# Turning normed rows over six PSUM banks, and the odd low halves of a layer norm on GpSimd

## What is computed

```python
h = rms_norm(h + merged @ w_out, norm_ffn)          # then h @ w_ffn_in: stage "ffn"
h = layer_norm(x, ln_in_g, ln_in_b)
for l in range(2):
    proj = h @ w_in[l]                              # stage "in" of layer l
    ...                                             # attention, mix
    h = layer_norm(ALPHA * h + mix, ln1_g[l], ln1_b[l])
    q = h @ wq[l]                                   # stage "exp" of layer l, then the experts
    ...
    h = layer_norm(ALPHA * h + ffn, ln2_g[l], ln2_b[l])
```

## Time and profile before

| what | value |
|---|---|
| median of 3 runs | 2452.79 us (2447.13 to 2454.69) |
| the profiled execution | 2454.43 us |
| its span, first to last instruction | 2452.6 us |
| mean granted clock of TensorE | 0.988 |
| TensorE busy | 2392.8 us (98%) |
| VectorE busy | 1676.7 us (68%) |
| ScalarE busy | 1264.9 us (52%) |
| GpSimd busy | 541.3 us (22%) |

### The profile page before, as it was taken

One profiled execution on the slowest core, in us unless ns is written; L12 is line 12 of the kernel. 1 busy time (PEld: TensorE's weight loads), 2 busy tenths in 40 slices (PEclk: granted clock), 3 DMA queues, 4 the chain that ended last, 5 costly groups with the idle time before them and its releaser, 6 DMA issues. The chain is left out here.

```text
span 2452.6 us, 42445 instructions
## 1 busy us (share of the span) xinstructions
PE 2392.8 (98%) x16695; PEld 2173.9 (89%) x16695; DVE 1676.7 (68%) x3016; ACT 1264.9 (52%) x2699; POOL 541.3 (22%) x423
## 2 busy tenths in 40 slices
PE   7999999999999999999999999999999999999997
PEld 7888989998889999999888878789999999888886
DVE  4737345446779767887777556769776888777556
ACT  6542335445655545445555555655554455555553
POOL 3640224545278200000000002368400000000000
PEclk9999999999899999999999999999999999999999
DMA  5320145554145566666777664245656666777664
GB/s 181 124 85 17 40 150 172 188 186 139 70 151 180 182 181 192 195 194 199 239 245 224 196 207 152 95 129 165 188 181 190 194 195 194 229 243 236 195 199 144
DMA packets 148068, 420.98 MB, mean 172 GB/s; under 512 B 15904, under 2 KB 49056, under 8 KB 147488
## 3 DMA queue, kind: packets, MB, share of 16 engines
q1 hardware_dynamic: 144080, 405.34, 52.8%
q0 software_dynamic: 2192, 8.99, 1.0%
q10 hardware_dynamic: 1600, 3.96, 0.5%
HBM read 400.40 MB, written 17.83 MB: 171 GB/s over the span
## 5 line engine op out<-in xcount | busy, mean ns | idle before, releaser
L1142 ACT CAST hi<-raw 128x512 fp32r<-128x512 f32 x1402 | 818.6, 620 | 379.9 <-PE pb L439 227.6
L439 PE MATMUL pb<-HTh,hi 128*128 128x256 f32 (+1 forms) x2968 | 857.6, 289 | 2.6 <-POOL lo L2377 1.9
L439 PE MATMUL pb<-HTl,hi 128*128 128x256 f32 (+1 forms) x2968 | 840.8, 283 | 0.0
L439 PE MATMUL pb<-HTh,lo 128*128 128x256 f32 (+1 forms) x2968 | 840.5, 283 | 0.0
L2377 POOL TENSOR_TENSOR lo<-raw,hi 128x512 fp32r<-128x512 f32 x383 | 520.7, 1383 | 542.1 <-ACT hi L1142 541.7
L1660 DVE TENSOR_TENSOR lo<-raw,hi 128x1024 fp32r<-128x1024 f32 x464 | 565.0, 1218 | 85.7 <-ACT hi L1142 85.5
L439 PEld LDWEIGHTS pb<-HTh,hi 128*128 128x128 f32 x2968 | 568.6, 192 | 7.2 <-issue 2.8
L439 PEld LDWEIGHTS pb<-HTl,hi 128*128 128x128 f32 x2968 | 569.1, 192 | 1.0
L439 PEld LDWEIGHTS pb<-HTh,lo 128*128 128x128 f32 x2968 | 568.6, 192 | 0.0
L439 PE MATMUL pb<-hi,WH 128*128 128x512 f32 x1112 | 433.5, 390 | 5.0 <-DVE WL L2341 4.9
L439 PE MATMUL pb<-lo,WH 128*128 128x512 f32 x1112 | 432.9, 389 | 0.0
(11 more groups left out here) (197 smaller groups left out, 2155.2 us busy)
## 6 DMA issues: line engine op xcount, KB each, us to landing
raw<-in_uT SPq DMA_DIRECT2D x256, 512.0 KB, 3.6
raw<-in_vT SPq DMA_DIRECT2D x256, 512.0 KB, 3.7
raw<-in_w_ffn_in SPq DMA_DIRECT2D x44, 512.0 KB, 4.0
raw<-in_wq SPq DMA_DIRECT2D x32, 512.0 KB, 3.5
wk<-kept SPq DMA_DIRECT2D x128, 128.0 KB, 3.8
raw<-in_w_in SPq DMA_DIRECT2D x24, 512.0 KB, 3.7
raw<-in_w_ffn_out SPq DMA_DIRECT2D x22, 512.0 KB, 4.3
raw<-in_w_gate SPq DMA_DIRECT2D x16, 512.0 KB, 3.3
```

The costliest lines, as they stand in the source:

```text
L439: return e.matmul(o, l, r, start=start, stop=stop)
L1142: e.copy(u.hi[k], u.half[k]).then_inc(*s.up("hi", ("hi", g)))
```

## The change

The table `NORMED` gives each kind of stage six banks and one spare bank for filler. On PE a new function `turned_normed` takes the place of `turned` in all five stages: chunks 0 to 5 go to six different banks, so none of them waits for a reader. Then come 8 filler matmuls, chunk 6 (first bank again), 3 filler matmuls, chunk 7 (second bank again) and 3 filler matmuls, and then the product. That is 14 filler matmuls in each stage that were not there.

In `in` and `exp`, POOL gets the low halves of the odd chunks 1, 3, 5, 7 (`turned_low`), ahead of its splits for the stage; DVE keeps those of 0, 2, 4, 6. ACT takes out the odd chunks 1, 3, 5 as before, and chunk 7 goes from ACT to DVE, which takes it out when `turn` of chunk 5 is there and its own low half of chunk 6 is done. Who waited for `turn` of chunk 7 now waits for that of 6 too, as the two are counted on different semaphores.

```diff
+NORMED = {"ffn": ((1, 2, 3, 4, 5, 6), 7), "in": ((0, 1, 2, 3, 6, 7), 5), "exp": ((2, 3, 4, 5, 6, 7), 1)}
...
+    def turned_normed(kind, tag, src, ready, done):
+
+        banks, other = NORMED[kind]
+        for c in range(8):
+            b = banks[c % 6]
+            if c == 6:
+                warm(other, 8)
+            elif c == 7:
+                warm(other, 3)
+            emptied(b)
+            for t in range(2):
+                w.wait_ge(*s.to(*ready(t, c // 4)))
+                x = tp(PB[b][:, t * 128:(t + 1) * 128], src[:, t, c * 128:(c + 1) * 128])
+            x.then_inc(*s.up("turn_ps", ("turn_ps", tag, c)))
+            free[b] = [(step, tag, c) for step in done]
+        warm(other, 3)
...
-    turned("ffn", m.XN, lambda t, k: ("xn1", t, k), range(8), FOUR)
+    turned_normed("ffn", "ffn", m.XN, lambda t, k: ("xn1", t, k), ("turn",))
...
-        turned(("in", l), m.Hv, lambda t, k: ("hn", 2 * l, t, k), range(8), FOUR, low=False)
+        turned_normed("in", ("in", l), m.Hv, lambda t, k: ("hn", 2 * l, t, k), ("biased",))
...
-        turned(("exp", l), m.Hv, lambda t, k: ("hn", 2 * l + 1, t, k), range(8), FOUR, low=False)
+        turned_normed("exp", ("exp", l), m.Hv, lambda t, k: ("hn", 2 * l + 1, t, k), ("biased",))
...
     def turned_biased(tag, gain, bias, prev):
 
+        banks = NORMED[tag[0]][0]
         for c in range(8):
-            p, h, ty = PB[c % 4][:, 0:256], m.HT[0][:, c, :], m.TY[c % 2]
-            if c % 2:
+            p, h, ty = PB[banks[c % 6]][:, 0:256], m.HT[0][:, c, :], m.TY[c % 2]
+            if c in (1, 3, 5):
                 w.wait_ge(*s.to("turn_ps", tag, c))
                 if c > 1:
                     w.wait_ge(*s.to("turn", tag, c - 2))
...
         def low(c):
             w.wait_ge(*s.to("turn_hi", tag, c))
-            x = tt(m.HT[1][:, c, :], m.TY[c % 2], m.HT[0][:, c, :].bitcast(F32), S)
-            x.then_inc(*up("turn", ("turn", tag, c), *(done if c == 7 else ())))
-
-        for c in range(8):
-            if c % 2 == 0:
-                w.wait_ge(*s.to("turn_ps", tag, c))
-                own()
-                ts(m.TY[0], PB[c % 4][:, 0:256], K(gain, c), K(bias, c), M, A).then_inc(*up("biased_dve", ("biased", tag, c)))
-            if c:
-                low(c - 1)
-        low(7)
+            x = tt(m.HT[1][:, c, :], m.TY[0], m.HT[0][:, c, :].bitcast(F32), S)
+            x.then_inc(*up("turn", ("turn", tag, c), *(done if c == 6 else ())))
+
+        banks = NORMED[tag[0]][0]
+        for c in (0, 2, 4, 6, 7):
+            w.wait_ge(*s.to("turn_ps", tag, c))
+            if c == 7:
+                w.wait_ge(*s.to("turn", tag, 5))
+            own()
+            ts(m.TY[c % 2], PB[banks[c % 6]][:, 0:256], K(gain, c), K(bias, c), M, A).then_inc(*up("biased_dve", ("biased", tag, c)))
+            if c < 7:
+                low(c)
...
+    def turned_low(tag):
+
+        for c in (1, 3, 5, 7):
+            w.wait_ge(*s.to("turn_hi", tag, c))
+            tt(m.HT[1][:, c, :], m.TY[1], m.HT[0][:, c, :].bitcast(F32), S).then_inc(*s.up("turn_pool", ("turn", tag, c)))
+
     for l in range(2):
+        turned_low(("in", l))
...
+        turned_low(("exp", l))
         for a in range(16):
             take("wq", l, a)
```

More of the change, by code:

```diff
@@ L1427, in scalar @@
     fn(sm[:, 64:66], sm[:, 62:64], ACT.Sqrt).then_inc(*s.up("roots", ("root1",)))
-    turned("ffn", range(8), FOUR, "norm_ffn")
+    turned("ffn", range(8), NORMED["ffn"][0], "norm_ffn")
     def ffn_in(j):
@@ L1577, in scalar @@
                 w.wait_ge(*s.to("key_ps", l, a - 2))
+            w.wait_ge(*s.to("turn", ("exp", l), 6))
             w.wait_ge(*s.to("turn", ("exp", l), 7))
@@ L1988, in gain_step @@
         w.wait_ge(*s.to("turn_ps", tag, 7))
+        w.wait_ge(*s.to("turn", tag, 6))
         w.wait_ge(*s.to("bc", n))
@@ L2432, in gpsimd @@
                 take("win", l, i, g)
+        w.wait_ge(*s.to("turn", ("in", l), 6))
         w.wait_ge(*s.to("turn", ("in", l), 7))
```

## The result

The change makes the kernel slower. Its median is 2461.34 us (2456.42 to 2463.74, 5 runs) against 2450.32 us of the kernel before, which five runs now have; the ratio is 1.0042, with an interval of [1.0026, 1.0058]. That is 6 to 14 us, where +2.9 us was forecast. In a second timing on another occasion it was 1.0048 [1.0035, 1.0062]. The median also lies 0.34 us over the upper end of the range. The forecast gave 91% to a change within 0.3%, and 1.0042 lies above that. That the median came so near the range is in part luck: the forecast started from a median of 2452.79 us, which five runs put at 2450.32. The two medians differ by 11.0 us, so the change itself was missed by 8.1 us, the time by 5.6 us only. And the two profiled executions differ by just 2.0 us.

The account below looks back on a forecast made before the run. The prediction took TensorE, busy 98% of the span, as the bound. Terms of +0.5 (`ffn`), +4.1 (`exp`) and -1.7 us (`in`) summed to +2.9: 2457.3 profiled, 2455.7 us as median, range 2449 to 2461.

Parts of the forecast that it names:

- The waits: In `exp`, TensorE's first product waits for chunk 3 until +4.65, 5 until +6.5 and 7 until +8.35 us.
- GpSimd's price: A 128x256 low half on POOL in `in` and `exp`: 0.72 us, with 0.45 and 1.26 as the ends.
- the longer chain: In `exp`, a pair of chunks takes 1.88 us instead of 1.55; the first product ends 0.6 us later.
- the half clock of `exp`: In each `exp`, 15 matmuls at 0.214 us instead of 0.12, later than before: 1.4 us.
- Transposes and filler: TensorE's transposes and filler take 3.8 to 4.0 us in each stage; in `ffn` this costs 0.5 us.
- `exp`, the term mis-sized: The two `exp` stages: later product end and half clock cost 2.0 us each, +4.1 us together.
- The rival that the clock holds: In `exp` the clock stays up despite the waits; the time is 2452.8 us; chance 17%.
- Term 3: The two `in` stages: no half clock, a 0.8 us wait for weights; gain 0.84 us each, -1.7 together.
- The base: Whole kernel: the profiled execution took 2454.43 us and the median of the runs lies 1.64 us below it.
- The rival on the slower side: POOL takes 1.26 us a low half in `in` and `exp`: +11.5 us, 2464.3 us; chance 5%.

Follow-up runs that it names:

- r9: The changed kernel with 39 instead of 3 filler matmuls behind chunk 7 in `exp`; 2456.74 us, ratio 1.0033 to the kernel before.
- r3: The changed kernel with four banks and no filler as before, keeping GpSimd's low halves and chunk 7 on VectorE; 2454.29 us, ratio 1.0027.
- r4: The change in the two `in` stages only, `ffn` and `exp` as in the kernel before; 2451.14 us, ratio 1.0017.
- r7: The change in the two `exp` stages only, `ffn` and `in` as in the kernel before; 2459.39 us, ratio 1.0038.
- r2: The changed kernel with six banks and filler, but all low halves on VectorE and chunk 7 on ScalarE as before; 2448.91 us, ratio 0.9991.
- r8: As r2, but `ffn` with four banks as before and 20 filler matmuls behind chunk 7 in `exp`; 2447.76 us, ratio 0.9994.
- r1: The changed kernel once more, without edit; 2458.62 us, ratio 1.0048 to the kernel before.

## Why the forecast was too low

The waits, GpSimd's price, the longer chain and the half clock of `exp` are in the traces where the forecast placed them. The gain in `in` is not there against the usual trace of before, and the sum was too small.

- **GpSimd's price** (0.72 taken, between 0.45 and 1.26): 0.72 to 0.74 measured. Right. That it contends with DVE was said but not priced: DVE's low halves beside it took 0.74 instead of 0.43, which put the last chunk at +8.71 and not at +8.3. The GPSIMD Engine Reference of the Trainium skill (Key points) names just this case, VectorE instructions with two SBUF inputs; the trace agrees with it. Its factor of about two for GpSimd (Engine selection) is 1.7 here, 0.73 against 0.43 us.
- **Transposes and filler.** 3.5 us from the first transpose to the product in `exp` (688.84 to 692.29) where 3.9 was taken; 3.2 in `in`. So `ffn` lost 0.15 us (9.57 against 9.42 to ACT's first step on the product), not 0.5. In `in`, on the other hand, TensorE came to the fifth chunk 0.35 us earlier than forecast and the weights 0.37 us later (+10.00 against +9.63), so it waited 1.57 us, not 0.8.
- **`exp`, the term mis-sized.** +2.0 each was forecast, +3.0 is the mean (15.2 of ten occurrences against 12.2), and +3.3 the usual value. The longer chain costs 1.1 (forecast 0.6). The half clock cost 2.2 (forecast 1.4): I let it last for 3.2 us of full work as in the trace of before, but it began before the last wait, and after that wait it lasted from 698.83 to 703.9, 5.1 us and 24 matmuls, not 15. The rival that the clock holds came true in one `exp` of ten.
- **`in`, the step that failed.** Term 3 was a gain of 0.84 us each, from half clock that the filler would take away. The forecast compared with a stage at half clock, since both `in` of the only trace had it. The other traces show it in one of six. With the clock up before, the stage took 14.4 us, and the change, which waits for weights instead, takes 15.6 to 15.8. Against the mean of the eight (15.0) the term is +0.7 each and not -0.84. I counted it as a gain that filler would bring, while it is mostly there without filler.
- **The base.** I corrected the profiled execution by 1.64 us to the median of three runs. Some 50 further runs of before had medians of 2448.3 to 2449.9, so the profiled execution of 2454.43 lies 4.5 to 6 us over the usual one.

The sum with the measured terms is 0.15 + 2 x 0.7 + 2 x 3.0 = 7.6 us, ratio 1.0031. It lies in the first interval [1.0026, 1.0058], a little under the second [1.0035, 1.0062]. Behind the first ffn transpose the three traces of the change are on the mean 6.0 us longer than the three of before (2078.3 against 2072.3), and 6.5 us longer (1884.5 against 1878.0) if the attention, which scatters with the clock, is taken off. That is near the 7.6, from three traces each.

Some 3 us of the timed difference are not accounted for. In r9 it is alike: 2 x 0.7 + 2 x 1.1 + 0.15 is 3.8 us, and 5 to 11 were timed. It is not alike in all: r3, r4 and r7, which also have GpSimd's low halves, were timed some 3 us over the sum of their stages too (6.6 against 3.6, 4.2 against 1.4, 9.3 against 6.6), and r2 and r8, which have none, were not (-2.2 against -2.3, -1.5 against -2.4). So the rest seems to come with GpSimd's low halves. The kept traces understate it: those of the change, of r1 and of r9 are the shortest executions of their five, six and nine. Of the eleven timed executions of the change, the four with a mean granted clock of 0.991 or 0.992 took 2453.3 to 2457.4 us, the seven with 0.988 to 0.990 took 2458.0 to 2463.7. So in the longer ones TensorE was at half clock for longer, and the attention, at 4.4 us a layer, is one place where that could be. Where it was is not shown, and this stays open. In r9 about 1 us more lies outside the span: its executions took 2.4 to 3.0 us longer than their spans, those of before 1.8.

The rival on the slower side (GpSimd at 1.26 us a low half) was the wrong mechanism for the right sign. GpSimd's low halves took 0.73 and not 1.26, and the slower `exp` came from DVE's contention and a longer half clock. The sensitivity that this rival names, 1.6 us for 0.1 us more on each low half, was not tried.

## What to carry to other kernels

Before a gain is booked for a stall that a trace shows, look at several traces: a half clock behind a thin stretch can be there in one execution and not in the next, and a forecast from one trace takes luck for a property. A step handed to an idle engine is not free when the buffer that it reads is the one that the next step needs: then the idle engine's time and two hand-overs are in the chain. Three more buffers gave back 0.7 us of that here, but the version without the idle engine was still shorter (11.70 against 12.6 us). And starting a product early is no gain if it then starves: with three waits of over 0.9 us each, the half clock came in nine stages of ten, and behind the last wait nothing covers it.

## What the runs showed of the hardware

The half clock lasted for 3.1 to 3.2 us of full work in some stages (695.13 to 698.29 in the first trace of before) and for longer in others: in the change from 697.26 to 703.90, of which 5.1 us, from 698.83 on, were full work. The same thin stretch, 2.73 us busy of 4, was followed by a granted clock of 0.53 in one execution and of 1.00 in another. DVE's subtraction of two SBUF operands took 0.74 to 0.76 instead of 0.43 us when it started 0.26 us behind GpSimd's, and 0.42 to 0.43 when it started 0.6 us behind it; GpSimd's own stayed at 0.72 to 0.75.
